# Splits of weights capped at two ahead of an operation, second feed-forward's first tiles interleaved, last mean first

## The chip, the core and the metric

The kernel runs on one NeuronCore of a Trainium2 chip. Its engines have an instruction queue each: PE multiplies matrices, ACT applies functions, DVE does elementwise arithmetic and reductions, POOL (GpSimd) a few helpers, SP issues most of the DMAs. Each works its own queue in order and waits for the others through semaphores. The metric is the device time of one execution in microseconds; lower is better.

## The reference

Two transformer blocks, one after the other, on 256 tokens of width 1024, in float32. Cut to what matters:

```python
mod = (silu(c) @ w_ada + b_ada).reshape(b, 3, 3, D)              # first block: shift, scale, gate per sub-layer
x = x + 0.5 * mod[0, 2] * swiglu(modulate(x, ...), w13[0], w2[0])  # first feed-forward, width 2816
x = x + mod[1, 2] * hybrid_mixer(modulate(x, ...))                 # latent attention, a convolution, gates, w_out
x = x + 0.5 * mod[2, 2] * swiglu(modulate(x, ...), w13[1], w2[1])  # second feed-forward
# second block
z = rmsnorm(x, g) @ w_in                                          # qa, ka, va, qb, kb, vb, two gates
x = x + (gate_a * (mixer_a(...) @ w_out_a) + gate_b * (mixer_b(...) @ w_out_b)) @ w_out
x = x + square(relu(rmsnorm(x, g) @ w_ff1)) @ w_ff2               # third feed-forward, width 4096
x = x + sigmoid(rmsnorm(x, g) @ w_ple_gate) * (p @ w_ple)
return rmsnorm(x, final_norm_g)
```

In the mixer `c_q`, `c_kv` and `k_rope` are columns of one product; queries and keys are made from their norms by `w_uq` and `w_ukv`, and are normed again by head before they are rotated.

## The kernel before

**Products in pieces.** PE multiplies in a rounded format (fp32r). To keep float32's precision, every weight is split into a rounded part (`whi`) and the rest (`wlo`), and so is every activation (`hh` and `hl`, or two halves of `SR`); a product is three matmuls (`mm3`, L462). The weights, some 200 MB, come as 331 pieces of at most 128x1024 elements, in the order in which PE takes them (class `Plan`). SP's queue loads two pieces with one DMA into one of four slots of `raw`. ACT then makes `whi` (`hi_to`, L1280 to L1287), DVE subtracts it from `raw` for `wlo` (`lo_to`, L1747 to L1755), and PE waits for that in `take` (L470). Both halves stand in a ring of `NP` = 6 pieces: ACT may write piece n only when PE is done with piece n - 6, and SP may load a slot again only when DVE has read it. A piece of 8 times 128 columns is 24 matmuls on PE.

**What sets the order.** Nothing schedules the splits at run time. `pe_program` is first run without emitting (its `count`, L477); at each signal that PE gives, it writes down in `split_at[key]` how many pieces may be split before and after the operation that waits for that key, from the pieces that PE has freed by then plus 6. `act_program` calls `hi_before(key)` ahead of an operation that waits for PE, `hi_after(key)` behind some. `dve_program` calls `lo_for(key)` likewise, and `after_act(key)`, which splits as many pieces as ACT had split by the time that it gave the key (`hi_at`), and then waits for ACT. All of these have a `most` with the default 99: they split to the ring's full. `lo_to(n)` in turn waits for ACT's `hi_done` of each piece.

**Stages around the change.** The first block's mixer runs from about 235 us: projections (`gate` tiles, then `c0`, `c1`), six more `gate` pieces (78 to 83), `uq` (84, 85), `ukv` (86), `cv` (87 to 98, convolution inputs, `back1` 3 to 8), and `gate` again (99 on). Between pieces 91 and 92 PE transposes the first 128 tokens' queries and keys, between 92 and 93 those of the other 128 (key `qkT`, with t, operand, half); DVE and ACT scale them out of PSUM by halves. DVE's loop over t norms and rotates queries and keys of one half of the tokens (`normed`).

The second feed-forward has 22 rows (`NT`). Tile r has a gate product and an up product; DVE scales both by the row `RB` (`g_in`, `u_in`), ACT applies silu (`sg`), DVE multiplies (`av`), ACT rounds that (`ah`), and DVE makes the rest (`a`); PE then multiplies them by a row piece of `w2`. PE does the gate and up products of tiles 0 to 3 before row 0. The buffers `W1`, `W2` hold three tiles.

At the end, after the third feed-forward, PE multiplies `ple` (pieces 321, 322; key ("ple", t, half)), sums the squares (`sums` 4), transposes `xT` back (two times eight), and takes the gate's pieces 323 to 330 in pairs. `token_rstd` (L1809) makes a mean and an inverse square root out of `sums` on DVE: one operation of 128x2 with the key `mean`, one of int32, seven small ones and a scaling.

Only the order of ACT's and DVE's instructions is changed; the orders of PE, SP and POOL are the same in both kernels.

## Time and profile before

| | |
|---|---|
| median of 3 runs | 1071.82 us (1071.53 to 1072.54) |
| profiled execution | 1072.67 us |
| its span | 1070.6 us |
| granted PE clock, mean | 0.985 |
| PE busy | 1029.1 us (96%) |
| DVE busy | 704.7 us (66%) |
| ACT busy | 538.2 us (50%) |

The profile is of one execution. The median stands 0.85 us under it. A clock of 1.00 is 2.4 GHz; the other level is 1.2 GHz. The page cuts the span into 40 slices, and in nearly all of them PE is at nine tenths or more; the stretches of interest are the few in which PE waits, and the splits on DVE there. Rows of a timeline that begin with the same operation are folded: "x6" is six instructions, and the time ahead of it is theirs together. The time in brackets is how long the engine stood idle before the row, and which instruction released it.

### The profile page before, as it was taken

To read this page: it belongs to the slowest core of one execution; us is meant where nothing else is said; L and a number is where in the kernel's file an instruction comes from. 1 tells how busy PE (TensorE), PEld (TensorE's weight loads), DVE (VectorE), ACT (ScalarE), POOL (GpSimd) and SP (SyncE) were. 2 spreads that over 40 slices of the span, in tenths; PEclk is the share of its full clock that TensorE was granted. 3 is DMA by queue.
4 is the path that set the end of the run, shared out by engine and by line. 5 is a ranking of instruction groups with operands and counts; after the bars stand their busy time and mean duration, and the time that the engine had idled before them with its cause. 6 is when DMAs were issued, how large, how long until landed. Compare 5 with 4: busy or idle time off the path is not lost.

```text
span 1070.6 us, 19826 instructions
## 1 busy us (share of the span) xinstructions
PE 1029.1 (96%) x8502; PEld 997.5 (93%) x8502; DVE 704.7 (66%) x1213; ACT 538.2 (50%) x903; POOL 39.0 (4%) x75
## 2 busy tenths in 40 slices
PE   5999999999989999799999999999999999999985
PEld 3899999988989999799999999999999999999975
DVE  3478886567686577677666778655467775555475
ACT  4453443445645555444444577554355564454543
POOL 5000000010000000000000000003000000000000
PEclk8999999999999999899999999999999999999988
DMA  9979889787553363567555456346157475555411
GB/s 305 379 261 331 293 317 333 266 276 239 165 159 118 122 200 102 202 243 275 183 191 188 128 187 209 117 137 159 60 168 231 163 236 197 186 169 197 159 40 40
DMA packets 144463, 212.27 MB, mean 198 GB/s; under 512 B 4259, under 2 KB 121239, under 8 KB 144376
## 3 DMA queue, kind: packets, MB, share of 16 engines
q1 hardware_dynamic: 138928, 194.40, 54.5%
q0 software_dynamic: 5184, 16.30, 4.8%
q8 instruction: 67, 1.10, 0.4%
q10 hardware_dynamic: 264, 0.31, 0.1%
q14 instruction: 20, 0.16, 0.0%
HBM read 209.88 MB, written 1.11 MB: 197 GB/s over the span
## 4 chain that ended last, share of the span: by engine, by line
PE 66%; issue 22%; DVE 5%; DMA 3%; ACT 2%; SPq 0%; POOL 0%; POOLq 0%; DVEq 0%; ACTq 0%
PE PS L460 65%; DMA SC<-in_w_ada_dram 3%; DVE wlo L1754 3%; PE PS L468 2%; ACT whi L1286 1%; DVE SC L1712 0%; DVE W L1712 0%; DVE xT L1721 0%; DVE st L1724 0%; ACT W L1273 0%; DVE hl L1721 0%; DVE SS L1712 0%; DVE st L1721 0%; DVE SC L1718 0%; ACT L1273 0%
## 5 line engine op out<-in xcount | busy, mean ns | idle before, releaser
L1754 DVE TENSOR_TENSOR wlo<-raw,whi 128x1024 fp32r<-128x1024 f32 (+2 forms) x331 | 385.4, 1187 | 218.7 <-ACT whi L1286 218.2
L1286 ACT ACTIVATE whi<-raw 128x1024 fp32r<-128x1024 f32 (+2 forms) x331 | 330.1, 1022 | 162.0 <-PE PS L460 125.4
L460 PE MATMUL PS<-hh,whi 128*128 128x256 f32 (+1 forms) x1376 | 394.2, 287 | 4.8 <-DVE wlo L1754 3.3
L460 PE MATMUL PS<-hh,wlo 128*128 128x256 f32 (+1 forms) x1376 | 389.2, 283 | 0.0
L460 PE MATMUL PS<-hl,whi 128*128 128x256 f32 (+1 forms) x1376 | 388.3, 282 | 0.0
L460 PE MATMUL PS<-SR,whi 128*128 128x256 f32 (+1 forms) x1824 | 330.9, 284 | 8.0 <-DVE W L1712 5.8
L460 PEld LDWEIGHTS PS<-SR,whi 128*128 128x128 f32 x1824 | 281.5, 189 | 12.5 <-DVE W L1712 6.0
L460 PEld LDWEIGHTS PS<-hh,whi 128*128 128x128 f32 x1376 | 260.6, 189 | 9.8 <-DVE wlo L1754 4.3
L460 PEld LDWEIGHTS PS<-hl,whi 128*128 128x128 f32 x1376 | 261.3, 190 | 0.4
L460 PEld LDWEIGHTS PS<-hh,wlo 128*128 128x128 f32 x1376 | 261.0, 190 | 0.0
L460 PE MATMUL PS<-SR,wlo 128*128 128x256 f32 (+1 forms) x912 | 257.8, 283 | 0.0
L460 PEld LDWEIGHTS PS<-SR,wlo 128*128 128x128 f32 x912 | 172.8, 190 | 0.0
L1278 ACT ACTIVATE SR<-W 128x256 fp32r<-128x256 f32 (+1 forms) x76 | 35.0, 461 | 93.6 <-DVE W L1721 51.9
L460 PE MATMUL PS<-whi,hh 128*128 128x256 f32 x240 | 69.4, 289 | 0.0
L460 PE MATMUL PS<-wlo,hh 128*128 128x256 f32 x240 | 68.1, 284 | 0.0
L460 PE MATMUL PS<-whi,hl 128*128 128x256 f32 x240 | 68.0, 283 | 0.0
L1712 DVE TENSOR_TENSOR SR<-W,SR 128x256 fp32r<-128x256 f32 (+1 forms) x76 | 36.5, 480 | 42.6 <-ACT SR L1278 42.6
L1273 ACT ACTIVATE W<-W 128x256 f32<-128x256 f32 (+1 forms) x38 | 21.3, 561 | 78.3 <-DVE W L1712 40.4
L460 PE MATMUL PS<-SC 128*64 128x128 f32 (+5 forms) x246 | 47.6, 336 | 0.0
L460 PEld LDWEIGHTS PS<-whi,hh 128*128 128x128 f32 x240 | 46.4, 193 | 0.6 <-DVE wlo L1754 0.4
L460 PEld LDWEIGHTS PS<-wlo,hh 128*128 128x128 f32 x240 | 46.4, 193 | 0.1
L460 PEld LDWEIGHTS PS<-whi,hl 128*128 128x128 f32 x240 | 46.3, 193 | 0.0
(183 smaller groups left out, 717.7 us busy)
## 6 DMA issues: line engine op xcount, KB each, us to landing
raw<-in_ffn_w_dram SPq DMA_DIRECT2D x60, 1024.0 KB, 5.5
raw<-in_w_in_dram SPq DMA_DIRECT2D x38, 1024.0 KB, 5.4
raw<-in_w_ff_dram SPq DMA_DIRECT2D x32, 1024.0 KB, 5.3
raw<-in_w_ada_dram SPq DMA_DIRECT2D x16, 1024.0 KB, 6.6
SC<-in_w_ada_dram POOLq DMA_DIRECT2D x12, 1024.0 KB, 5.8
SC<-in_w_ada_dram SPq DMA_DIRECT2D x8, 1024.0 KB, 12.0
raw<-in_w_out_dram SPq DMA_DIRECT2D x8, 1024.0 KB, 4.8
raw<-in_ffn_w_dram SPq DMA_DIRECT2D x8, 768.0 KB, 12.9
```

Source lines behind the costliest of these rows:

```text
L460: return e.matmul(o, l, r, start=start, stop=stop, skip_group_check=True)
L468: return e.transpose(o, i, ident[0:p, 0:p])
L1273: e.activation(o, i, f, bias=bias, scale=scale, accum_out=acc).then_inc(*act_done.up(*keys))
L1278: e.activation(o, i, ACT.Copy, scale=scale).then_inc(*act_done.up(*keys))
L1286: e.activation(hi_part(p), raw_part(p), ACT.Copy).then_inc(*hi_done.up(p.i))
L1712: e.tensor_tensor(o, x, y, op).then_inc(*dve_done.up(*keys))
L1754: e.tensor_tensor(lo_part(p), raw_part(p), hi32(hi_part(p)), ALU.subtract).then_inc(*lo_done.up(p.i))
```

## The change

- `split_at[key]` has a third number: how many pieces PE has already taken at that signal, which have to be split by then. `hi_before` and `lo_for` split these, and beyond them at most `most` pieces, now 2 by default, never past the ring's full. `lo_for` goes only as far as ACT had gone at its own `hi_before` of the same key (`high_by`); where ACT has none for the key, only the pieces already taken are left. `after_act` splits at most `most` (2) for all its keys together. Some calls have a `most` of 0 or 1.
- In the mixer the run of splits after each half's scaling (`lo_to(hi_at["qkT", 1, t])`) goes, and calls for ("ukv", t) and ("back1", 3 + t) come in.
- In the second feed-forward the steps of tiles 0, 1 and 2 are interleaved on ACT and DVE, and the up product is scaled right behind the gate product in all tiles.
- In the third feed-forward ACT may split behind the square.
- The last mean and root (`token_rstd(4, 3)`) stand ahead of the copies of `ple`, and a split between these.

```diff
--- before.py
+++ after.py
@@ -325,7 +325,7 @@
         every_signal = [mm_done, hi_done, lo_done, act_done, dve_done, pool_done, *raw_in, *row_in, *pair_in, c_in, *x_in, sv_in,
                         rel_in, hot_in, pos_in, sw_in, inv_in, cs_in, gb_in, rel_out, pin_in, gfin_in, out_done,
                         *out_lo, *bias_in]
-        split_at, hi_at = {}, {}
+        split_at, hi_at, high_by = {}, {}, {}
 
         def hi32(v):
             return v.bitcast(F32)
@@ -480,7 +480,7 @@
                 while used["free"] in used["done"]:
                     used["free"] += 1
                 for k in keys:
-                    split_at[k] = before, used["free"] + NP
+                    split_at[k] = used["n"], before, used["free"] + NP
                 return mm_done.up(*keys)
 
             def halves(p, k):
@@ -1286,11 +1286,12 @@
                     e.activation(hi_part(p), raw_part(p), ACT.Copy).then_inc(*hi_done.up(p.i))
                     high["n"] += 1
 
-            def hi_before(key, most=99):
-                hi_to(min(split_at[key][0], high["n"] + most))
-
-            def hi_after(key, most=99):
-                hi_to(min(split_at[key][1], high["n"] + most))
+            def hi_before(key, most=2):
+                hi_to(max(split_at[key][0], min(split_at[key][1], high["n"] + most)))
+                high_by[key] = high["n"]
+
+            def hi_after(key, most=2):
+                hi_to(min(split_at[key][2], high["n"] + most))
 
             def modulated(s, ks, free=None, ahead=(), piece_key=None):
                 for k in ks:
@@ -1531,16 +1532,29 @@
             hi_before(("g", 1, 0))
             on.wait_ge(mm_done, ("rstd_row", 2))
             copy(RB[:, 0:S], PS[:, 1, 0:S], ("RB", 2))
-            for r in range(NT):
+            def gate_on(r):
                 hi_before(("g", 1, r))
                 on.wait_ge(dve_done, ("g_in", 1, r))
                 sg = W1[:, r % 3, :]
                 func(sg[:, 0:S], sg[:, 0:S], ACT.Silu, ("sg", 1, r), bias=sg[:, S:S + 1])
                 hi_before(("u", 1, r))
+
+            def high_activated(r):
                 on.wait_ge(dve_done, ("av", 1, r))
                 if r >= 6:
                     on.wait_ge(mm_done, ("row", 1, r - 6))
                 copy(aring[r % 6][0], W2[:, r % 3, 0:S], ("ah", 1, r))
+
+            gate_on(0)
+            gate_on(1)
+            hi_before(("u", 1, 2))
+            high_activated(0)
+            gate_on(2)
+            high_activated(1)
+            high_activated(2)
+            for r in range(3, NT):
+                gate_on(r)
+                high_activated(r)
             ada_rows_out(8, 6, 0, ("ada_sum", 8))
             hi_before(("row", 1, NT - 4))
             for n in range(8):
@@ -1667,6 +1681,7 @@
                 hi_before(("f", j, 1))
                 on.wait_ge(dve_done, ("f_in", j))
                 func(W2[:, j % 3, :], W1[:, j % 3, :], ACT.Square, ("f_sq", j))
+                hi_after(("f", j, 1))
                 if j >= 4:
                     on.wait_ge(mm_done, ("row", 3, 2 * j - 7))
                 on.wait_ge(act_done, ("f_sq", j))
@@ -1754,12 +1769,11 @@
                     e.tensor_tensor(lo_part(p), raw_part(p), hi32(hi_part(p)), ALU.subtract).then_inc(*lo_done.up(p.i))
                     low["n"] += 1
 
-            def lo_for(key, most=99):
-                lo_to(min(split_at[key][0], low["n"] + most))
-
-            def after_act(*keys):
-                for k in keys:
-                    lo_to(hi_at[k])
+            def lo_for(key, most=2):
+                lo_to(max(split_at[key][0], min(high_by.get(key, 0), low["n"] + most)))
+
+            def after_act(*keys, most=2):
+                lo_to(min(max(hi_at[k] for k in keys), low["n"] + most))
                 on.wait_ge(act_done, *keys)
 
 
@@ -2140,22 +2154,24 @@
                 vcopy(k_sb[:, t, :, 64:96], kr.to_broadcast([128, HEADS, 32]), ("kr", t))
             lo_to(hi_at["back1", 2])
             for t in range(2):
-                after_act(("k_raw", t))
+                lo_for(("ukv", t), 1)
+                after_act(("k_raw", t), most=1)
                 src = PS[:, 4 + 2 * t:6 + 2 * t, :].rearrange("p g (h c) -> p g h c", h=4)
                 vcopy(v_sb[:, t, :].rearrange("p (g h c) -> p g h c", g=2, h=4), src[:, :, :, 64:128], ("k_in", t))
             for t in range(2):
-                after_act(("q_sq", t))
+                after_act(("q_sq", t), most=0)
                 qs = W1f[:, 768 * t:768 * t + 768].rearrange("p (h c) -> p h c", c=QKD)
                 reduce(ssq[:, 0, t, :], qs[:, :, 0:64], ALU.add)
                 reduce(ssq[:, 2, t, :], qs[:, :, 64:96], ALU.add)
             for t in range(2):
-                after_act(("k_sq", t))
+                after_act(("k_sq", t), most=0)
                 reduce(ssq[:, 1, t, :], W2f[:, 512 * t:512 * t + 512].rearrange("p (h c) -> p h c", c=64), ALU.add)
             last_one()
             ts(st[:, 88:120], st[:, 40:72], 1.0 / 64, EPS, ALU.mult, ALU.add)
             ts(st[:, 120:136], st[:, 72:88], 1.0 / 32, EPS, ALU.mult, ALU.add)
             rsqrt(st[:, 88:136], st[:, 136:184], st[:, 184:232], st[:, 40:88])
             for t in range(2):
+                lo_for(("back1", 3 + t), 1)
                 def of_head(a_, n):
                     return rs1[:, a_, t, :].unsqueeze(2).to_broadcast([128, HEADS, n])
 
@@ -2167,11 +2183,10 @@
                 tt(k_sb[:, t, :, 0:64], k_sb[:, t, :, 0:64], of_head(1, 64), ALU.mult, ("normed", 1, t))
             for t in range(2):
                 for i, (dst, g) in enumerate(((qT, gq96), (kT, gk96))):
-                    lo_for(("qkT", t, i, 0))
+                    lo_for(("qkT", t, i, 0), 1)
                     on.wait_ge(mm_done, ("qkT", t, i, 0))
                     ts1(dst[:, 0:4, 128 * t:128 * t + 128], PS[0:96, 4 + 2 * i, :].rearrange("p (h c) -> p h c", h=4), g, ALU.mult,
                         ("qkT", i, t))
-                lo_to(hi_at["qkT", 1, t])
                 if t:
                     read_back1([3, 4])
 
@@ -2231,25 +2246,44 @@
             lo_for(("sums", 1))
             token_rstd(1, 0)
             spread_rstd(1, ("rstd_row", 1))
-            for r in range(NT):
+            def gate_and_up(r):
                 sg, av = W1[:, r % 3, :], W2[:, r % 3, :]
                 g, u = ((4, 5), (6, 7), (2, 3))[r] if r < 3 else (4, 5) if r % 2 else (6, 7)
                 lo_for(("g", 1, r))
                 if r == 0:
-                    after_act(("RB", 2))
+                    after_act(("RB", 2), most=0)
                     on.wait_ge(pool_done, "one")
                 on.wait_ge(mm_done, ("g", 1, r))
                 if r >= 3:
                     on.wait_ge(dve_done, ("a", 1, r - 3))
                 tt(sg[:, 0:S + 1], PS[:, g, 0:S + 1], RB[:, :], ALU.mult, ("g_in", 1, r))
-                lo_for(("u", 1, r))
+                lo_for(("u", 1, r), 0)
                 on.wait_ge(mm_done, ("u", 1, r))
                 tt(av[:, 0:S + 1], PS[:, u, 0:S + 1], RB[:, :], ALU.mult, ("u_in", 1, r))
+
+            def activated(r):
+                sg, av = W1[:, r % 3, :], W2[:, r % 3, :]
                 after_act(("sg", 1, r))
-                last_one()
+                on.wait_ge(dve_done, ("u_in", 1, r))
                 stt(av[:, 0:S], av[:, 0:S], av[:, S:S + 1], sg[:, 0:S], ALU.add, ALU.mult, ("av", 1, r))
+
+            def low_activated(r):
                 after_act(("ah", 1, r))
-                tt(aring[r % 6][1], av[:, 0:S], hi32(aring[r % 6][0]), ALU.subtract, ("a", 1, r))
+                tt(aring[r % 6][1], W2[:, r % 3, 0:S], hi32(aring[r % 6][0]), ALU.subtract, ("a", 1, r))
+
+            gate_and_up(0)
+            gate_and_up(1)
+            activated(0)
+            gate_and_up(2)
+            activated(1)
+            low_activated(0)
+            activated(2)
+            low_activated(1)
+            low_activated(2)
+            for r in range(3, NT):
+                gate_and_up(r)
+                activated(r)
+                low_activated(r)
             after_act(("ada_rows", 8))
             lo_for(("ada_col", 8))
             mod_half(8, 6, 0)
@@ -2402,11 +2436,12 @@
 
 
 
-            lo_for(("ple", 1, 1))
-            for t in range(2):
+            lo_for(("ple", 1, 1), 0)
+            token_rstd(4, 3)
+            for t in range(2):
+                lo_for(("ple", t, 1), 1)
                 on.wait_ge(mm_done, ("ple", t, 0))
                 vcopy(ple[:, t, 0:512], PS[:, 4 + 2 * t, :], ("ple", t))
-            token_rstd(4, 3)
             on.wait_ge(gfin_in, "gfin")
             for u in range(4):
                 for t in range(2):
```

The rows below are DVE's instructions in the order of its queue. `wlo<-raw,whi` is the low half of a piece; "x2" is two instructions alike. The first place is the mixer's loop over the two halves of the tokens, where products with `st` are norms and those with `rtab` rotations, and 96x4x128 is the scaling of transposed queries and keys. Before:

```order
L1712 TENSOR_TENSOR SC<-SC,rtab 128x8x32
L1712 TENSOR_TENSOR SC<-SC,W2 128x8x32
L1712 TENSOR_TENSOR SC<-SC,st 128x8x64
L1712 TENSOR_TENSOR SC<-SC,st 128x8x32
L1712 TENSOR_TENSOR SC<-SC,st 128x8x64
L1712 TENSOR_TENSOR W2<-SC,rtab 128x8x16 x2
L1712 TENSOR_TENSOR SC<-SC,rtab 128x8x32
L1712 TENSOR_TENSOR SC<-SC,W2 128x8x32
L1712 TENSOR_TENSOR SC<-SC,st 128x8x64
L1754 TENSOR_TENSOR wlo<-raw,whi 128x1024 x6
L1718 TENSOR_SCALAR SC<-PS,svt 96x4x128 x2
L1754 TENSOR_TENSOR wlo<-raw,whi 128x1024
```

After:

```order
L1727 TENSOR_TENSOR SC<-SC,rtab 128x8x32
L1727 TENSOR_TENSOR SC<-SC,W2 128x8x32
L1727 TENSOR_TENSOR SC<-SC,st 128x8x64
L1769 TENSOR_TENSOR wlo<-raw,whi 128x1024 x2
L1727 TENSOR_TENSOR SC<-SC,st 128x8x32
L1727 TENSOR_TENSOR SC<-SC,st 128x8x64
L1727 TENSOR_TENSOR W2<-SC,rtab 128x8x16 x2
L1727 TENSOR_TENSOR SC<-SC,rtab 128x8x32
L1727 TENSOR_TENSOR SC<-SC,W2 128x8x32
L1727 TENSOR_TENSOR SC<-SC,st 128x8x64
L1769 TENSOR_TENSOR wlo<-raw,whi 128x1024
L1733 TENSOR_SCALAR SC<-PS,svt 96x4x128 x2
```

The six low halves ahead of the scalings (pieces 92 to 97) are gone; two (89 and 90) stand behind the first half's norm, one (91) ahead of the scalings. Before, 89 to 91 stood ahead of this stretch, together with 88.

The second place is the start of the second feed-forward, from the spread of the root (`sm<-ones,sm`). `W1<-PS,RB` and `W2<-PS,RB` are the gate's and the up product's scaling, `W2<-W2,W1` their product, `SR<-W2,SR` its low half. Before:

```order
L1715 TENSOR_SCALAR sm<-ones,sm 128x128 x2
L1712 TENSOR_TENSOR W1<-PS,RB 128x257
L1754 TENSOR_TENSOR wlo<-raw,whi 128x1024
L1712 TENSOR_TENSOR W2<-PS,RB 128x257
L1721 SCALAR_TENSOR_TENSOR W2<-W2,W1 128x256
L1712 TENSOR_TENSOR SR<-W2,SR 128x256
L1754 TENSOR_TENSOR wlo<-raw,whi 128x1024
L1712 TENSOR_TENSOR W1<-PS,RB 128x257
L1754 TENSOR_TENSOR wlo<-raw,whi 128x1024
L1712 TENSOR_TENSOR W2<-PS,RB 128x257
L1721 SCALAR_TENSOR_TENSOR W2<-W2,W1 128x256
L1712 TENSOR_TENSOR SR<-W2,SR 128x256
```

After:

```order
L1730 TENSOR_SCALAR sm<-ones,sm 128x128 x2
L1769 TENSOR_TENSOR wlo<-raw,whi 128x1024 x2
L1727 TENSOR_TENSOR W1<-PS,RB 128x257
L1727 TENSOR_TENSOR W2<-PS,RB 128x257
L1769 TENSOR_TENSOR wlo<-raw,whi 128x1024 x2
L1727 TENSOR_TENSOR W1<-PS,RB 128x257
L1727 TENSOR_TENSOR W2<-PS,RB 128x257
L1736 SCALAR_TENSOR_TENSOR W2<-W2,W1 128x256
L1769 TENSOR_TENSOR wlo<-raw,whi 128x1024 x2
L1727 TENSOR_TENSOR W1<-PS,RB 128x257
L1727 TENSOR_TENSOR W2<-PS,RB 128x257
L1736 SCALAR_TENSOR_TENSOR W2<-W2,W1 128x256
```

The scalings of three tiles now come before the third product, and the first low half of an activation stands behind the third tile's scalings.

The third place is the last mean, `sm<-PS`; `SC<-PS 128x512` is a copy of `ple`. Before:

```order
L1721 SCALAR_TENSOR_TENSOR hl<-xT,svt,hh 128x256
L1754 TENSOR_TENSOR wlo<-raw,whi 128x1024 x3
L1709 COPY SC<-PS 128x512 x2
L1715 TENSOR_SCALAR sm<-PS 128x2
L1715 TENSOR_SCALAR sm<-sm 128x2
L1721 SCALAR_TENSOR_TENSOR sm<-sm 128x1 x2
L1721 SCALAR_TENSOR_TENSOR sm<-sm 128x2
L1721 SCALAR_TENSOR_TENSOR sm<-sm 128x1 x2
L1721 SCALAR_TENSOR_TENSOR sm<-sm 128x2 x2
L1718 TENSOR_SCALAR sm<-sm 128x2
L1754 TENSOR_TENSOR wlo<-raw,whi 128x1024 x2
```

After:

```order
L1736 SCALAR_TENSOR_TENSOR hl<-xT,svt,hh 128x256
L1730 TENSOR_SCALAR sm<-PS 128x2
L1730 TENSOR_SCALAR sm<-sm 128x2
L1736 SCALAR_TENSOR_TENSOR sm<-sm 128x1 x2
L1736 SCALAR_TENSOR_TENSOR sm<-sm 128x2
L1736 SCALAR_TENSOR_TENSOR sm<-sm 128x1 x2
L1736 SCALAR_TENSOR_TENSOR sm<-sm 128x2 x2
L1733 TENSOR_SCALAR sm<-sm 128x2
L1724 COPY SC<-PS 128x512
L1769 TENSOR_TENSOR wlo<-raw,whi 128x1024
L1724 COPY SC<-PS 128x512
L1769 TENSOR_TENSOR wlo<-raw,whi 128x1024 x3
```

The mean and the root went ahead of all splits and copies; the piece that PE takes with the first pair (324) stands behind them and one copy.

## Rows read from the trace of the kernel before

**Rows 1.** The page: busy time and share, PE.

```profile
PE 1029.1 (96%) x8502; PEld 997.5 (93%) x8502; DVE 704.7 (66%) x1213; ACT 538.2 (50%) x903; POOL 39.0 (4%) x75
```


**Rows 2.** The page: the chain that ended last, by engine.

```profile
PE 66%; issue 22%; DVE 5%; DMA 3%; ACT 2%; SPq 0%; POOL 0%; POOLq 0%; DVEq 0%; ACTq 0%
```


**Rows 3.** The page: the splits' low halves, 331; busy and mean ns, idle before.

```profile
L1754 DVE TENSOR_TENSOR wlo<-raw,whi 128x1024 fp32r<-128x1024 f32 (+2 forms) x331 | 385.4, 1187 | 218.7 <-ACT whi L1286 218.2
```


**Rows 4.** Waits of PE from 60 us on: total, times, longest (us).

```profile
PE PS L460 <- DVE W L1712: 5.8, 1, 5.8
PE PS L468 <- DVE sm L1715: 5.2, 1, 5.2
...
PE PS L460 <- DVE wlo L1754: 0.4, 1, 0.4
```


**Rows 5.** Timeline of PE: start us, us, what, [idle before <- releaser].

```profile
266.24 0.39 PE L460 MATMUL PS<-hh,whi 128*128 128x256 f32 x1 [1.01 <-DVE SC L1718]
...
290.99 0.28 PE L460 MATMUL PS<-hh,wlo 128*128 128x256 f32 x1
...
299.67 1.91 PE L468 MATMUL PS<-ident,SC 128*96 128x128 f32 x16
...
308.39 3.33 PE L468 MATMUL PS<-ident,SC 128*96 128x128 f32 x16 [3.31 <-DVE SC L1718]
...
439.82 0.79 PE L460 MATMUL PS<-SR,whi 128*128 128x256 f32 x2 [5.83 <-DVE W L1712]
```


**Rows 6.** Windows: length, busy of PE, PEld, DVE, ACT, POOL, clock, DMA.

```profile
300.00:320.00 20.00, 16.30 (x124) 15.65 (x123) 16.79 (x25) 10.46 (x17) 0.00 (x0) 0.91 0.68 211
440.00:460.00 20.00, 20.00 (x151) 20.00 (x152) 14.54 (x20) 9.55 (x14) 0.00 (x0) 0.89 0.63 223
```


**Rows 7.** Timeline of DVE in the first block's mixer.

```profile
234.21 3.10 DVE L1754 TENSOR_TENSOR wlo<-raw,whi 128x1024 fp32r<-128x1024 f32 x3
238.68 0.16 DVE L1715 TENSOR_SCALAR sm<-PS 128x2 f32<-128x2 f32 x1 [1.37 <-PE PS L460]
...
240.64 0.48 DVE L1715 TENSOR_SCALAR sm<-ones,sm 128x128 f32<-128x128 f32 x2
...
284.61 3.50 DVE L1754 TENSOR_TENSOR wlo<-raw,whi 128x1024 fp32r<-128x1024 f32 x3 [5.51 <-ACT whi L1286]
...
296.98 1.75 DVE L1712 TENSOR_TENSOR SC<-SC,st 128x512 f32<-128x512 f32 x3
...
300.69 6.89 DVE L1754 TENSOR_TENSOR wlo<-raw,whi 128x1024 fp32r<-128x1024 f32 x6
307.50 1.40 DVE L1718 TENSOR_SCALAR SC<-PS,svt 96x512 f32<-96x512 f32 x2
...
316.13 1.22 DVE L1754 TENSOR_TENSOR wlo<-raw,whi 128x1024 fp32r<-128x1024 f32 x1
```


**Rows 8.** Timeline of DVE in the projections by token.

```profile
637.36 2.35 DVE L1754 TENSOR_TENSOR wlo<-raw,whi 128x1024 fp32r<-128x1024 f32 x2
```


**Rows 9.** Timeline of DVE at the second feed-forward's start.

```profile
422.89 0.43 DVE L1712 TENSOR_TENSOR W<-PS,RB 128x257 f32<-128x257 f32 x1 [1.22 <-ACT RB L1278]
...
436.27 0.42 DVE L1712 TENSOR_TENSOR W<-PS,RB 128x257 f32<-128x257 f32 x1
...
439.35 0.42 DVE L1712 TENSOR_TENSOR W<-PS,RB 128x257 f32<-128x257 f32 x1
```


**Rows 10.** Timeline of PE at the last mean.

```profile
1027.41 1.07 PE L468 MATMUL PS<-ident,xT 128*128 128x128 f32 x8
1033.63 1.97 PE L468 MATMUL PS<-ident,xT 128*128 128x128 f32 x8 [5.16 <-DVE sm L1715]
```


**Rows 11.** Timeline of DVE at the last mean.

```profile
1028.82 3.50 DVE L1754 TENSOR_TENSOR wlo<-raw,whi 128x1024 fp32r<-128x1024 f32 x3 [1.79 <-ACT whi L1286]
1032.23 1.28 DVE L1709 COPY SC<-PS 128x512 f32<-128x512 f32 x2
1033.43 0.15 DVE L1715 TENSOR_SCALAR sm<-PS 128x2 f32<-128x2 f32 x1
```


## The prediction

> **What bounds the kernel now.** I read the profile's page first. PE is busy 96% of the span [rows 1], and the chain that ended last is PE for 66% and issue for 22% [rows 2], so what counts is each microsecond in which PE stands still or runs at the lower clock. DVE and ACT have room on average: a piece of weights, once ACT has rounded it, takes DVE 1.19 us for what is left [rows 3], against 24 matmuls at 0.119 us, 2.85 us, on PE. So an edit of DVE's or ACT's order costs nothing unless PE arrives at a piece whose split is not there. Then the waits of PE behind the opening stage: 5.8 us once on the products of the second feed-forward, 5.2 us once on the last mean, 0.4 us once on a split [rows 4]; the others are in PE's timeline below: 3.3 us once on the scaled queries, and a few of 1 us or less. These are where a gain can lie.
>
> The windows and PE's timeline say what a stall costs beyond its length. After 1.01 us of idle at 266.24 the next matmuls keep their 0.12 us pace; after 3.31 us at 308.39 sixteen transposes take 3.33 us where sixteen took 1.91 at 299.67, so 1.4 us more; after 5.83 us at 439.82 the window 440:460 shows a granted clock of 0.89 with PE never idle: 11% of 20 us, 2.2 us [rows 5, 6]. There are two levels, 2.4 and 1.2 GHz, and half the time spent at the lower is lost. I price a stall of 1 us at its length, one of 5 to 6 us at its length plus 1.7 (between 1.4 and 2.2), and one of 2 us with 0 to 1.4 more, taking 0.6.
>
> **First block's mixer: the cap takes splits out of slack.** Before, DVE split to the end of the ring of six wherever it might. Now at most two come ahead of an operation, and for a key at which ACT never asked (("back1", 3), ("qkT", t, i, 0)) only the pieces that PE has already taken. Five places come out of it.
> - Piece 73: before, DVE split 73 to 75 in 234.21 to 237.31 and then had 1.37 us idle before the mean at 238.68; mean, root and spread end at 241.1 [rows 7]. Now the split stands behind them and ends at 241.1 + 1.2 = 242.3, where PE wants it at about 240.8: +1.5. In return the five splits that held the root of the latent's norm go behind it, and the stall of 1.01 [rows 5] goes: together +0.5.
> - Piece 85: it now stands behind the rotation of the keys (two rounds, about 2.0 us of small operations); PE wants it 1.4 us sooner: +1.4.
> - Piece 89, the largest: before, 89 to 91 were split at 284.61 to 288.11, in an idle of 5.51 us, ahead of the copies, squares' sums, root and first rotation that end with the 296.98 row's first operation (0.68 us: 297.66) [rows 7]. Now 89 and 90 stand behind that. ACT asks two pieces instead of three before its copies (-0.95) but starts 1.4 later, so the chain ends at 298.1 and the split at 299.3. PE finishes piece 88 at 291.27 [rows 5] + 1.9 from the two items above = 293.2: a stall of 6.1, and 1.7 of clock, +7.8.
> - Piece 92: behind the first two scalings (0.70 each, 1.40 for both at 307.50), [rows 7], the second of which waits for the third quarter of the transposes, a quarter of 1.91 us before PE wants the piece: 0.70 + 1.2 - 0.48 = 1.4.
> - Piece 93: before, split in the run of six at 300.69, now where piece 99 stood: behind both scalings, the sum with ACT's copy and four products, which ended so that its split ran at 316.13 for 1.22 us, to 317.35 [rows 7]. The second sixteen transposes ended at 308.39 + 3.33 = 311.72, after which PE wants the piece: 5.6, and 1.7 of clock, +7.3.
> - Gone: that run of six (6.89 us) ahead of the scalings, so the 3.31 stall, its 1.4 of clock, and the 0.4 at piece 92 [rows 4]: -5.1.
>
> Sum 0.5 + 1.4 + 7.8 + 1.4 + 7.3 - 5.1 = +13.3. Ends: +10 if the chain before 89 starts 2 us sooner and the clock falls once, +17 if the shorter stalls too cost clock.
>
> **Second block's projections by token.** The pairs of splits at 637.36 (2.35 us) and after are in the same place, but each now trails a rotation by one piece more [rows 8]. I get 0.5 at the keys, 1.6 at the queries and 0.2 to 0.5 at a turn, +2.3; from 0 (each has a row of DVE idle of 0.5 to 2.8 us within 10 us before it) to +4.
>
> **Start of the second feed-forward.** Before, each of the first tiles r goes DVE, ACT, DVE, ACT, DVE in turn; from tile 0's first scaling at 422.89 to tile 2's at 436.27 are two rounds, 6.69 us each, and PE waits until tile 2's second scaling at 439.35 is done [rows 9]. Now both scalings of tile 1 and then of tile 2 come between the steps of tile 0. In the durations of [rows 9]: spread, two splits (2.4), scalings of 0 (0.8), two splits, scalings of 1, a product, two splits, scalings of 2: 421.7 + 7.2 (six splits) + 2.5 + 0.5 = about 431.7, and the tile 0 product's low half near 433.5. PE is ready at 433.99 before, and 0.3 earlier as the spread moves ahead of a split. So the stall of 5.83 and its 2.2 of clock go [rows 5, 6]: -8.3, between -5 (2.8 us left, with clock) and -8.8. Later tiles have 14 us of room per piece: the cap costs nothing there.
>
> **The way into the third feed-forward** has a 0.94 stall of which half stays: -0.5.
>
> **The last mean.** Before, DVE ran three splits at 1028.82 and two copies at 1032.23 before the mean at 1033.43, and PE idled 5.16 us ahead of the second eight transposes [rows 10, 11]. Now the mean goes at once, 1027.6, and the transposes go on to 1029.3. Then PE wants piece 324, whose split is behind mean and root (1.83, the rows' 1033.43 to 1035.26) and one copy (0.6): 1027.6 + 1.83 + 0.6 + 1.2 = 1031.3. So a stall of 2.0 takes the place of 5.16: the gate's matmuls start at 1031.3 instead of 1035.26, -3.95, and at 0.119 instead of 0.213 us until 1038.4, up to 1.4 more. I take -4.6; the tail of 11 us after the last piece keeps its length.
>
> A rule bears on that 1.4. Before, eight transposes on the way took 1.97 us after the stall against 1.07 before it [rows 10]. The Trainium skill, "TensorE: Matmul & The Clock Gate", Part 4 (PE-mode transpose), says that a transpose does not count as busy for the clock gate. By that rule the transposes and the 2.0 us behind them are one quiet stretch, the gate's matmuls start slow as before, and this part gives -4.0 rather than -5.4. No row here shows transposes followed by a stall of this length.
>
> **Sum.** 13.3 + 2.3 - 8.3 - 0.5 - 4.6 = +2.2 us. The profiled execution took 1072.67, so 1074.9 in its terms; it stood 0.85 above the median of 1071.82, so I predict 1074.0 in the terms of the median. By the ends: 1071.82 + 10 + 0 - 8.8 - 0.5 - 5.4 = 1067.1, and 1071.82 + 17 + 4 - 5 - 4 = 1083.8.
>
> **Rivals.**
> 1. Faster: the front gives less. The by-token pairs fall into their idle (-2.3), piece 85 is hidden behind the longer run of PE (-1.4), and the clock does not fall a second time at piece 93 (-1.7): 1068.6. For it: DVE is busy for 66% only, and 16.79 of 20 us in the window 300:320 held 8 splits that now leave it. Against: 89 and 93 stand behind long serial chains whatever the load.
> 2. Slower: each new stall of 1.4 to 2 us lowers the clock as well. Four places at 1.1 each: 1078.4. For it: 3.31 us did. Against: 1.01 us did not. It decides from where between the two the clock falls.
> 3. Slower: the interleaving leaves half of the 5.8 us, since tile 0's last product waits behind six splits and tile 2 behind ACT's; 3 us stay, with the 2.2 of clock: 1079.2. Against: each of the splits was there before too, in the idle time of the DVE.
> 4. The change does nothing for the mixer, because a piece that PE has taken and one that it is about to take differ by one position only: then +2.2 - 13.3, 1060.7. Against: the order of DVE's instructions has piece 89 behind the whole norm.
>
> **Chances.** Forecast (1071 to 1077) 0.42; rival 1 0.25; rival 2 0.17; rival 3 0.10; rival 4 and the rest 0.06. A measurement can tell about 0.2% from no change, so faster means below 1069.7 and slower above 1074.0. Faster: three quarters of rival 1, and rival 4: 0.22. Same: the rest of rival 1 and half of the forecast: 0.27. Slower: the rest, 0.51. The range leaves out rival 4 and the far part of rival 3: 1067.5 to 1079.5; the forecast's own is 1071 to 1077.
>
> **What would show it.** PE waits of 5 to 6.5 us on a split twice between 290 and 325, with clocks under 1 in two windows there; waits of 1 to 2 us at the two short places before and at 640; no wait over 1 us at the start of the second feed-forward and window 440:460 at 1.00; at the end one wait of 2 us on a split. The prediction is wrong if the wait at piece 89 is under 4 us or if a stall over 2 us remains at 434.

## The result, and the profile after

| | before | changed |
|---|---|---|
| median | 1072.18 us (1071.53 to 1073.11, 4 runs) | 1083.24 us (1082.89 to 1085.34, 4 runs) |
| ratio | | 1.0107, 95% interval [1.0089, 1.0124] |
| profiled execution, its span | 1072.67, 1070.6 | 1083.11, 1081.1 |
| granted PE clock, mean | 0.985 | 0.981 |

The change makes the kernel 11 us slower. The forecast was 2 us slower, with a range up to 1079.5, so the time lies outside. The page of the changed kernel shows PE busy for the same share of the span and DVE for a little less (64% for 66%); as before [rows 1, 3], averages say nothing here:

```profile
PE 1033.6 (96%) x8502; PEld 999.4 (92%) x8502; DVE 696.9 (64%) x1213; ACT 531.7 (49%) x903; POOL 39.1 (4%) x75
```

The view of PE's waits from 60 us on answers to [rows 4]. Total, times and longest are in us:

```profile
PE PS L460 <- DVE wlo L1769: 24.0, 12, 5.9
```

The three long waits of before (5.8, 5.2, 3.3 us, each on another result) are gone. In their place stand twelve on one thing, the low half of a piece. PE's timeline of the changed kernel has them one by one, and answers to [rows 5, 10]:

```profile
91.62 0.58 PE L460 MATMUL PS<-hh,whi 128*128 128x256 f32 x1 [2.68 <-DVE wlo L1769]
...
99.61 0.39 PE L460 MATMUL PS<-hh,whi 128*128 128x256 f32 x1 [0.62 <-DVE wlo L1769]
...
103.23 0.39 PE L460 MATMUL PS<-hh,whi 128*128 128x256 f32 x1 [0.52 <-DVE wlo L1769]
...
248.34 0.50 PE L460 MATMUL PS<-SR,whi 128*128 128x258 f32 x2 [1.41 <-DVE wlo L1769]
...
286.58 0.42 PE L460 MATMUL PS<-whi,SR 128*128 128x384 f32 x1 [1.61 <-DVE wlo L1769]
...
294.16 0.39 PE L460 MATMUL PS<-hh,whi 128*128 128x256 f32 x1 [0.31 <-DVE wlo L1769]
...
305.97 0.58 PE L460 MATMUL PS<-hh,whi 128*128 128x256 f32 x1 [5.86 <-DVE wlo L1769]
...
319.74 0.39 PE L460 MATMUL PS<-hh,whi 128*128 128x256 f32 x1 [1.54 <-DVE wlo L1769]
...
330.29 0.58 PE L460 MATMUL PS<-hh,whi 128*128 128x256 f32 x1 [5.69 <-DVE wlo L1769]
...
649.70 0.39 PE L460 MATMUL PS<-whi,hh 128*128 128x256 f32 x1 [0.44 <-DVE wlo L1769]
...
656.99 0.39 PE L460 MATMUL PS<-whi,hh 128*128 128x256 f32 x1 [1.38 <-DVE wlo L1769]
...
1045.57 0.36 PE L460 MATMUL PS<-whi,hh 128*128 128x256 f32 x1 [1.98 <-DVE wlo L1769]
```

The rows from 248 on are pieces 73, 85, 87, 89, 92 and 93, two of the projections by token, and 324, all places that the prediction names except 87. The first three, in the first feed-forward, are in no term of it. The windows tell where the clock was low, as in [rows 6]; 440:460, which stood at 0.89 before, is at 1.00:

```profile
80.00:100.00 20.00, 16.70 (x127) 16.30 (x126) 9.93 (x13) 3.64 (x5) 0.00 (x0) 0.91 0.45 153
300.00:320.00 20.00, 12.61 (x92) 12.24 (x91) 13.34 (x27) 3.64 (x6) 0.00 (x0) 0.83 0.18 54
320.00:340.00 20.00, 14.31 (x106) 13.96 (x106) 10.70 (x18) 10.47 (x17) 0.00 (x0) 0.83 0.35 105
440.00:460.00 20.00, 19.88 (x167) 19.70 (x166) 15.29 (x25) 11.61 (x18) 0.00 (x0) 1.00 0.43 158
1040.00:1060.00 20.00, 18.02 (x136) 17.54 (x135) 13.63 (x28) 9.47 (x17) 0.00 (x0) 0.91 0.00 1
```

I then took the same operations of PE in both traces, since PE's order is the same, and noted by how much the changed kernel is later at each (the up product of the first feed-forward's tile 8 ends at 106.35, before at 100.35: 6.0). The lateness grows and shrinks in steps. The second feed-forward is counted from the spread of its root on, as in the prediction:

| place | lateness at its end, us | step | forecast |
|---|---|---|---|
| first feed-forward, tiles 7 and 8 | 6.0 | +6.0 | none |
| first block's mixer | 20.4 | +14.3 | +13.3 |
| start of the second feed-forward, with its spread | 12.0 | -8.4 | -8.3 |
| projections by token | 14.9 | +2.9 | +2.3 |
| into the third feed-forward | 14.2 | -0.7 | -0.5 |
| last mean | 10.4 | -3.8 | -4.6 |

Before rounding the steps add up to 10.4; the spans differ by 10.5.

A stall makes PE later by about 0.25 us more than its idle time, also where the clock does not fall: the wait of 1.41 us is a step of 1.66, that of 1.38 a step of 1.64. The rows show why. At full pace a matmul lasts 0.28 us and the next one starts 0.12 us after it, so the idle time is counted from an end that lies 0.16 us behind the next start, and the first matmul behind a stall lasts up to 0.39 us and not 0.28.

**What happened in the first feed-forward.** ACT's timeline of the kernel before, from 73 to 92 us: it rounds four pieces in a row (22 to 25) and then waits 7.2 us for a load. The two loads that bring pieces 26 to 29 are issued from 81.73 on, when DVE has made the low halves of 24 and 25 (the first line, from SP's timeline).

```profile
81.73 1.50 SPq L1198 DMA_DIRECT2D raw<-in_ffn_w_dram  x2
...
75.88 3.90 ACT L1286 ACTIVATE whi<-raw 128x1024 fp32r<-128x1024 f32 x4
86.97 1.06 ACT L1286 ACTIVATE whi<-raw 128x1024 fp32r<-128x1024 f32 x1 [7.20 <-DMA raw<-in_ffn_w_dram]
90.49 2.01 ACT L1286 ACTIVATE whi<-raw 128x1024 fp32r<-128x1024 f32 x2 [2.45 <-DMA raw<-in_ffn_w_dram]
```

ACT's timeline of the changed kernel, the same stretch: two pieces (22, 23), then it stands idle for 11.1 us in front of the silu of tile 6, which waits for PE's product out of piece 23. Only then are 24 and 25 rounded, when PE already wants 24.

```profile
75.89 2.00 ACT L1286 ACTIVATE whi<-raw 128x1024 fp32r<-128x1024 f32 x2
88.98 0.38 ACT L1273 ACTIVATE W<-PS 128x256 f32<-128x256 f32 x1 [11.10 <-PE PS L460]
89.26 1.99 ACT L1286 ACTIVATE whi<-raw 128x1024 fp32r<-128x1024 f32 x2
...
96.72 1.06 ACT L1286 ACTIVATE whi<-raw 128x1024 fp32r<-128x1024 f32 x1 [5.17 <-DMA raw<-in_ffn_w_dram]
100.86 1.06 ACT L1286 ACTIVATE whi<-raw 128x1024 fp32r<-128x1024 f32 x1 [3.07 <-DMA raw<-in_ffn_w_dram]
```

The rest follows down the line. DVE, which waits for ACT's half, makes the low halves of 24 and 25 late; with each of them a slot of `raw` comes free, so SP issues the next two loads from 91.60 on and not from 81.73:

```profile
90.34 2.36 DVE L1769 TENSOR_TENSOR wlo<-raw,whi 128x1024 fp32r<-128x1024 f32 x2 [0.52 <-ACT whi L1286]
...
91.60 1.50 SPq L1198 DMA_DIRECT2D raw<-in_ffn_w_dram  x2
```

So ACT rounds piece 26 at 96.72 (before: 86.97) and 27 at 100.86 (before: 90.49). PE pays 2.68 us, 1.7 us of lower clock and of restart, then 0.62 and 0.52, and 0.5 for these two restarts: 6.0. Tile 6 is the first whose gate and up products come from the stream of pieces; those of tiles 0 to 5 come from the opening pieces 0 to 15, long done when ACT asks. Why the cap costs nothing more in the tiles behind 8 stays open.

### The profile page after: what moved, and what is told of

Same layout as the page of the kernel before. It is cut to its first block, busy times and chain, and to the rows that moved or that the text cites. A ratio compares the mean times of both kernels' runs of the same rounds, so it can differ in the third digit from the quotient of the medians.

```text
span 1081.1 us, 19808 instructions
## 1 busy us (share of the span) xinstructions
PE 1033.6 (96%) x8502; PEld 999.4 (92%) x8502; DVE 696.9 (64%) x1213; ACT 531.7 (49%) x903; POOL 39.1 (4%) x75
## 4 chain that ended last, share of the span: by engine, by line
PE 68%; issue 22%; DVE 6%; DMA 2%; ACT 2%; SPq 0%; POOL 0%; POOLq 0%; DVEq 0%
PE PS L460 66%; DVE wlo L1769 2%; PE PS L468 2%; DMA SC<-in_w_ada_dram 1%; DMA raw<-in_ffn_w_dram 1%; DVE SC L1727 1%; ACT SC L1278 1%; ACT whi L1286 1%; DVE xT L1736 0%; DVE W L1727 0%; DVE hl L1736 0%; DVE st L1739 0%; ACT W L1273 0%; DVE SS L1727 0%; DVE SC L1724 0%
## 5 line engine op out<-in xcount | busy, mean ns | idle before, releaser
L1727 DVE TENSOR_TENSOR W<-PS,RB 128x257 f32<-128x257 f32 x44 | 18.0, 423 | 46.7 <-PE PS L460 45.4
```

What stands on the lines that cost most here:

```text
L1727: e.tensor_tensor(o, x, y, op).then_inc(*dve_done.up(*keys))
```

## The experiments

Each ran beside the kernel before, so a ratio stands beside every time. The time of the kernel before differed between the occasions: its median was 1072.2 us beside the changed kernel, 1073.2 beside e1 to e4, 1073.6 beside e5 to e8 and 1073.7 beside e9 and e10. The expectations were written in plain times, so these are compared first; where it matters, the difference by the ratios stands beside them, in us of 1072.2. Base is either the changed kernel or the kernel before. The diffs show the lines that matter, with dots for the others. Theory A throughout: the places don't influence each other, and each costs what its stall and its clock cost.

**e1: the first feed-forward's splits uncapped.** The changed kernel with a switch; where it is on, `hi_before`, `hi_after`, `lo_for` and `after_act` take the limits of before. It is on around ACT's loop, shown here, and around DVE's.

```diff
+            full["on"] = True
             for r in range(NT):
                 swiglu0(r)
...
+            full["on"] = False
             on.wait_ge(dve_done, (("h", 0), 7))
```

> The changed kernel, but with the splits of the first feed-forward (ACT and DVE) to the ring's full, as before the change. Theory A (the costs of the places are independent and add up): the stalls of 2.68, 0.62 and 0.52 us that the changed kernel shows between 91 and 104 us, and the 1.7 us at the lower clock behind the first, go, and nothing takes their place: about 1083.2 - 6.0 = 1077.2 us, with all the later stalls unchanged. Rival B (the cap's lateness is passed on: a stall that goes at one place comes back at the next one, since DVE and ACT are as late as before): less than half of it comes back, 1080.5 or more.

Measured: 1077.01 us (1075.56 to 1078.66, 8 runs), ratio to before 1.0037 [1.0025, 1.0049]. That is 6.2 us less than the changed kernel (7.5 by the ratios, 1.0107 and 1.0037, with an interval of 5.2 to 9.8, which holds the 6.0). In its profile nothing is waited for between 60 and 240 us, and the other waits on pieces are as they were (PE, all from 60 us on: nine instead of twelve):

```profile
PE PS L461 <- DVE wlo L1776: 20.2, 9, 5.9
```

The same operations of PE are 6.0 us earlier than in the changed kernel behind this place. Farther on the two profiles differ by their clock alone, with the same waits: 1.0 us more is lost to it in the mixer and 1.5 us less at the last mean. So the missing term is this one, and rival B falls: nothing is passed on.

**e2: the mixer's splits as before.** The same switch around the mixer, on ACT too; there the run behind the scalings comes back, and the new calls for ("ukv", t) and ("back1", 3 + t) drop out.

```diff
+            full["on"] = True
             lo_for(("sums", 0))
             token_rstd(0, 0)
...
+                lo_to(hi_at["qkT", 1, t])
                 if t:
                     read_back1([3, 4])
+            full["on"] = False
```

> The changed kernel, but with the splits of the first block's mixer, from its first mean to the second half's scalings, in the order of before the change. Theory A: stalls of 1.41, 1.61, 0.31, 5.86, 1.54 and 5.69 us go and the ones of before (1.01, 0.38, 3.31) return with their clock: 13.8 us less, 1083.2 - 13.8 = 1069.4 us, so faster than the kernel before. Rival B: half of it or less, 1076 or more.

Measured: 1070.25 us (1066.93 to 1073.46, 10 runs), ratio 0.9972 [0.9959, 0.9985]: 13.0 us less than the changed kernel, 14.5 by the ratios. The forecast was 13.8 less, so A holds and B falls. The stalls of before came back (1.01, 0.38, 3.31), with one new wait of 0.43 us at 254.18. The profiled execution is the fastest of the ten, and odd in its clock, told of at the end.

**e3: the interleaving alone**, on the kernel before. ACT's and DVE's loops over the first three tiles are those of the changed kernel, the splits go to the ring's full; only the call between the gate's and the up product's scaling is left out (the changed kernel has it with a `most` of 0).

```diff
-            for r in range(NT):
...
+            gate_and_up(0)
+            gate_and_up(1)
+            activated(0)
+            gate_and_up(2)
+            activated(1)
+            low_activated(0)
...
```

> The kernel before with one part of the change alone: the first three tiles of the second feed-forward interleaved on ACT and DVE, every split to the ring's full as before. Theory A: the 5.8 us wait and its 2.2 us at the lower clock go, 1072.2 - 7.8 = 1064.4 us (between 1063.8 and 1065). Rival C (the interleaving pays only since the cap keeps the splits out of these steps): the third tile's scaling is still late behind the splits to the ring's full, 2 to 3 us of the wait stay, with the lower clock: 1067 to 1069.

Measured: 1063.86 us (1062.62 to 1064.59, 4 runs), ratio 0.9911 [0.9894, 0.9927]. The 5.8 us wait is gone from its list of waits, of which the first four are:

```profile
PE PS L468 <- DVE sm L1728: 5.2, 1, 5.2
PE PS L468 <- DVE SC L1731: 3.3, 1, 3.3
PE PS L460 <- DVE SC L1731: 1.0, 1, 1.0
PE PS L460 <- DVE xT L1725: 0.9, 1, 0.9
```

Rival C falls: the interleaving doesn't need the cap of two. DVE's timeline of e3 shows two splits between the tiles, as in the changed kernel, although `most` is unlimited: DVE waits for ACT's half at each pair (1.19 and 0.80 us), so ACT has no more pieces to give there.

```profile
423.21 0.76 DVE L1725 TENSOR_TENSOR W<-PS,RB 128x257 f32<-128x257 f32 x2 [1.22 <-ACT RB L1278]
425.16 2.36 DVE L1767 TENSOR_TENSOR wlo<-raw,whi 128x1024 fp32r<-128x1024 f32 x2 [1.19 <-ACT whi L1286]
427.44 0.75 DVE L1725 TENSOR_TENSOR W<-PS,RB 128x257 f32<-128x257 f32 x2
428.11 0.48 DVE L1734 SCALAR_TENSOR_TENSOR W<-W 128x256 f32<-128x256 f32 x1
429.38 2.36 DVE L1767 TENSOR_TENSOR wlo<-raw,whi 128x1024 fp32r<-128x1024 f32 x2 [0.80 <-ACT whi L1286]
431.66 0.75 DVE L1725 TENSOR_TENSOR W<-PS,RB 128x257 f32<-128x257 f32 x2
```

The third tile's scalings end at 432.4, where they ended at 439.8 before [rows 9]; the prediction had 431.7.

**e4: the last mean alone**, on the kernel before.

```diff
-            lo_for(("ple", 1, 1))
+            token_rstd(4, 3)
             for t in range(2):
                 on.wait_ge(mm_done, ("ple", t, 0))
                 vcopy(ple[:, t, 0:512], PS[:, 4 + 2 * t, :], ("ple", t))
-            token_rstd(4, 3)
+                if not t:
+                    lo_for(("ple", 1, 1), 1)
+            lo_for(("ple", 1, 1))
```

> The kernel before with another part of the change alone: the last mean and root ahead of the copies and splits. Theory A: the 5.2 us wait becomes one of 2.0 us on piece 324, and the clock falls all the same: 1072.2 - 3.9 = 1068.3 us. Rival D (the clock falls because of the length of the gap alone, and 2.0 us are not enough): no matmul at the lower pace behind it, 1.5 us more: 1066.8.

Measured: 1068.44 us (1067.28 to 1070.67, 5 runs), ratio 0.9961 [0.9945, 0.9977]. The wait of 5.16 became one of 1.98 us, and the lower pace is there (PE's timeline; from 1031.09 on each matmul lasts 0.41 us and not 0.28, and the next one starts 0.21 us later and not 0.12):

```profile
1026.61 1.94 PE L468 MATMUL PS<-ident,xT 128*128 128x128 f32 x16
1030.53 0.35 PE L460 MATMUL PS<-whi,hh 128*128 128x256 f32 x1 [1.98 <-DVE wlo L1754]
1030.73 0.28 PE L460 MATMUL PS<-wlo,hh 128*128 128x256 f32 x1
...
1030.96 0.33 PE L460 MATMUL PS<-whi,hh 128*128 128x256 f32 x1
1031.09 0.41 PE L460 MATMUL PS<-wlo,hh 128*128 128x256 f32 x1
```

So A holds here, in time (1068.3) and in the clock. Rival D's price, no fall of the clock behind the same gap, is seen in the profiles of e1 and e2; the last section has both.

**e5 and e10: both gains on the kernel before**, with the mean's operation alone first and the root behind the copies.

```diff
...
+            ts(sm[:, 272:272 + n], PS[:, 3, 0:n], 1.0 / D, EPS, ALU.mult, ALU.add, ("mean", 4))
             for t in range(2):
                 on.wait_ge(mm_done, ("ple", t, 0))
                 vcopy(ple[:, t, 0:512], PS[:, 4 + 2 * t, :], ("ple", t))
+                if not t:
+                    lo_for(("ple", 1, 1), 1)
+            last_one()
+            rsqrt_columns(sm[:, 272:272 + n], rsy[:, 0:n], sm[:, 276:276 + n], n)
...
```

> The kernel before with the two paying parts: the tiles of the second feed-forward interleaved, and at the end the mean alone first (one operation), then a copy, the split of piece 324, the other copy, and only then the root. Theory A (the stalls add up, and at the end PE waits for piece 324 and not for the root): the wait ahead of the gate's matmuls is 0.7 us instead of 2.0, so 1063.9 (interleaving alone) - 4.7 (last mean alone) - 1.3 = 1057.9 us, and 1056.4 if the clock no longer falls. Rival: the root is needed there after all, or the piece's high half is late; then the wait stays near 2 us: 1059.2.

> The kernel of e5_both_gains once more, unchanged, on the chip of the run beside it, for comparison: 1057.6 us.

Measured: 1057.58 us (1056.79 to 1058.98, 4 runs), ratio 0.9850 [0.9835, 0.9866]; again, on another occasion, 1058.88 us, ratio 0.9866 [0.9843, 0.9888]. PE's wait ahead of the gate's matmuls is 0.80 us (forecast 0.7):

```profile
1022.86 0.36 PE L460 MATMUL PS<-whi,hh 128*128 128x256 f32 x1 [0.80 <-DVE wlo L1767]
```

PE needs the mean only since it has to be read before the second eight transposes overwrite it. The root is needed by ACT, which first reads it 5.7 us after the mean (1025.98 for 1020.29) and waits there for PE, not for DVE. The changed kernel put the whole chain ahead. In both profiles the matmuls behind the 0.80 us keep the full pace, and for that case A had 1056.4; in plain times the two runs stand 1.2 and 2.5 us above it, by the ratios (1056.1 and 1057.8) at it and 1.4 above. This rest is unexplained.

**e6: the keys that ACT doesn't have.** The changed kernel, the cap as it is; for the keys ("back1", 3) and ("qkT", ...) the limit is the ring's, not 0.

```diff
-                lo_to(max(split_at[key][0], min(high_by.get(key, 0), low["n"] + most)))
+                lo_to(max(split_at[key][0], min(high_by.get(key, split_at[key][1] if key[0] == "qkT" or key == ("back1", 3) else 0), low["n"] + most)))
```

> The changed kernel, where lo_for has for the keys (back1, 3) and (qkT, t, i, 0), at which ACT never asked, the old limit instead of 0; the cap stays at two or one pieces. It puts piece 89 ahead of the first half's norm instead of behind it, and pieces 93 and 94 between the second half's scalings. Theory A (the two long stalls of the mixer come from the keys that ACT doesn't have, not from the size of the cap): piece 89's wait 5.86 - 3.1 (norm and rotation of a half) = 2.8, piece 92's 0.8, piece 93's gone with its 1.7 us of clock: 11.2 to 12.9 us less, 1070.3 to 1072.0. Rival E (the cap of two itself is what delays them): the waits move to the pieces behind, less than 5 us gained, 1078 or more.

Measured: 1073.76 us (1072.06 to 1074.84, 10 runs), ratio 0.9999 [0.9990, 1.0008]. In plain times that is 9.5 us less than the changed kernel and 1.8 us above the upper end of A; by the ratios it is 11.6 us less, which is inside A (11.2 to 12.9). Rival E falls either way. PE's timeline has the waits for pieces 89, 91 and 92:

```profile
302.60 0.39 PE L460 MATMUL PS<-hh,whi 128*128 128x256 f32 x1 [2.76 <-DVE wlo L1769]
...
310.85 0.39 PE L460 MATMUL PS<-hh,whi 128*128 128x256 f32 x1 [0.78 <-DVE wlo L1769]
...
316.37 0.38 PE L460 MATMUL PS<-hh,whi 128*128 128x256 f32 x1 [0.66 <-DVE wlo L1769]
```

Piece 89 is as A has it (2.76 for 2.8), and so is 92 (0.66 for 0.8, behind the first transposes at 313.79). Piece 93's wait is gone. A had not counted piece 91, which now waits 0.78 us, nor two waits of 0.3 us on ACT in the attention. Set side by side, PE's operations in the two profiles give 11.6 us for pieces 89, 92 and 93, less 1.0 for piece 91 and 1.3 for the attention: 9.3 of the mixer's 14.3. The larger part of the mixer's loss, then, is not the number two: it is that a key unknown to ACT gives DVE nothing beyond what PE has taken already.

**e7: a filler.** e4, and 16 matmuls whose result is overwritten, between the two sets of transposes.

```diff
                 if t:
+                    for k in range(KD):
+                        on.wait_ge(dve_done, (("xs1", 4), k))
+                        for i in range(2):
+                            mm(PS[:, 2, 0:256], hh[:, k, 0:128], hh[:, k, 0:256], True, True)
                     on.wait_ge(dve_done, ("mean", 4))
```

> The kernel with the last mean alone moved (e4_last_mean_only) and 16 matmuls of 128x256 with no use between the two sets of eight transposes; their result is overwritten. They fill the 1.98 us in which PE waited for piece 324 (16 x 0.119 = 1.9). Theory F (transposes and the gap together lower the clock): the gate's matmuls stay at 0.119 us, and 1068.4 - 1.5 = 1066.9 us. Rival G (the fall has another cause than idle time and transposes): 1068.4, with the lower pace still there. If they delay the transposes more than they fill: 1069 or more.

Measured: 1067.63 us (1066.50 to 1069.72, 6 runs), ratio 0.9946 [0.9931, 0.9961] against e4's 0.9961 [0.9945, 0.9977]. The intervals overlap, so the time decides nothing. In its profile no wait is left there and the gate's matmuls go at 0.12 us from the start; but see the last section for why one profile doesn't decide it.

**e8 and e9: a cap only where a run stands ahead of what PE waits for.** e5, with

```diff
-            lo_for(("ada_col", 6))
+            lo_for(("ada_col", 6), 4)
...
-            after_act("c_sq")
+            on.wait_ge(act_done, "c_sq")
...
-                    lo_for(("qkT", t, i, 0))
+                    lo_for(("qkT", t, i, 0), 2 if (t, i) == (0, 0) else 0)
...
-                lo_to(hi_at["qkT", 1, t])
+                lo_to(min(hi_at["qkT", 1, t], low["n"] + 3))
```

(this is e9; e8 has no 4 in the first call, so that piece 83 is still split ahead of the root and the 1.01 us wait stays, and a 2 instead of the 3).

> The kernel of e5_both_gains, and in the mixer a cap only where a run of splits stands ahead of what PE waits for: two splits instead of six ahead of the first half's scalings, two behind each half's, and the sum of squares' root not behind piece 83. Theory A: the waits of 1.0 and 3.3 us go and at most 0.5 us comes instead; 4.3 us less than e5, and 1.4 more where the clock fell: 1052.2 to 1053.6 us. Rival B: the pieces held back are late themselves (94 to 98), as those of the changed kernel were, and half or more comes back: 1055.5 or more.

> The kernel of e8_mixer_trimmed with two corrections: piece 83 is now split behind the root of the latent's norm (in e8 another call still split it ahead, and the 1.01 us wait stayed), and three pieces instead of two are split behind each half's scalings, so that one less stands ahead of the first scores, where e8 showed new waits of 1.06 and 1.03 us. Theory A: the wait at 266 goes (-1.0) and of the 2.4 us of new waits at least 1 goes: 1056.3 - 2.0 = 1054.3 us. Rival B (what is taken from one queue place is late at the next): the sum of the waits between 260 and 335 us stays near 3.8 us, 1056.3.

Measured: e8 1056.32 us (1055.86 to 1057.12, 4 runs), ratio 0.9838 [0.9824, 0.9852]. e9 1055.91 us (1055.47 to 1056.35, 4 runs), ratio 0.9835 [0.9818, 0.9853], the fastest of all, 3.0 us under e10 beside it. The intervals of these two ratios touch, but the times themselves, four of each, do not: 1055.47 to 1056.35 against 1058.00 to 1060.07. Those of e8 and e5, again beside each other, do (1055.86 to 1057.12, 1056.79 to 1058.98), so e8's gain is not clear of noise. For e8 the time is rival B's (1055.5 or more), but not its cause: in the mixer PE waits for one low half, 0.39 us, as it did before, and for none of the pieces that are held back. E9 lies nearer B's 1056.3 than A's 1054.3; of A's two steps the first came (the wait at 266 is gone) and the second did not. PE's timeline of e9 in the mixer's attention:

```profile
320.55 0.55 PE L468 MATMUL PS<-ident,SC 128*128 128x128 f32 x3 [1.05 <-DVE SC L1731]
...
325.64 0.52 PE L468 MATMUL PS<-ident,SC 128*128 128x128 f32 x3 [1.03 <-ACT SC L1278]
...
330.97 0.52 PE L468 MATMUL PS<-ident,SC 128*128 128x128 f32 x3 [0.33 <-ACT SC L1278]
```

The waits of 1.0 and 3.3 us are gone, and 2.4 us of new ones stand in the attention, on results of DVE and ACT, which PE now reaches sooner. The third split behind the scalings changed none of them (1.06, 1.03, 0.32 in e8). Their cause stays open, and so does whether a split's place could shorten them.

## Why the prediction was wrong, step by step

- **The missing step: the first feed-forward.** The prediction has no term for it; it costs the cap in "later tiles" of the second one at nothing, by their 14 us of room, and says of the first nothing at all. It cost +6.0, and e1, which undoes that place alone, gives 6.2 back. The room was there in the first one as well, for DVE and ACT as a sum; what was not counted is that an in-order engine that waits for PE can't use it. The silu stands in front of the splits, and it waits for the product out of the last piece that had been split. With this term the forecast is 1074.0 + 6.0 = 1080.0, 3.2 us under the measured 1083.2. The other steps together were 2.2 off (the table, before rounding: 1.0 - 0.1 + 0.6 - 0.1 + 0.8), the median of before went from 1071.8 to 1072.2, and the medians differ by 11.1 where the spans differ by 10.5.
- **The mixer** was right in mechanism and nearly in size: 14.3 against 13.3. Piece 73: 1.41 (1.5). 85: 1.61 (1.4). 89: 5.86 (6.1). 92: 1.54 (1.4). 93: 5.69 (5.6). Piece 87's 0.31 was overlooked, and so was the 0.25 us that a stall costs beyond its length: three more stalls than before make 0.75. Undone alone (e2), it gives 13.0 in plain times, 14.5 by the ratios.
- **The second feed-forward's start:** -8.4 against -8.3. Of it 7.8 are the stall with its clock (forecast 8.0) and 0.6 the spread (0.3). Alone, it gives 9.5 us by e3's ratio, whose interval reaches from 7.8 to 11.4.
- **By token:** +2.9 against +2.3; the waits are 0.44 and 1.38 (0.5 and 1.6), each with 0.25 for the restart.
- **The last mean:** -3.8 against -4.6. The wait was 1.98 (2.0). The term that was off is the clock: I took 0.6 us of the 1.4 as won, and in that profile nothing of it was.
- **Rivals.** Rival 1 (less in the front) and 3 (half of the 5.8 stays) are refuted by the waits, rival 4 by pieces 89 and 93. Rival 2 is on the side where the time went, for another reason: the waits of 1.4 to 1.6 us lowered no clock (the granted clock behind each stays at 1.00, and the steps are about 0.25 us over the waits), the one of 2.68 did.
- **The range** did not hold the time, though the ends of the terms, 1067.1 to 1083.8, do. The upper end needed every part at its worst: 17 in the mixer, 4 by token, 3.3 us of the second feed-forward's gain lost. Each of these stayed short of it, and the 6.0 us that stood in no term made up for them, so it is chance that 1083.2 lies under 1083.8. The range itself was narrower, to 1079.5, since it left out rival 4 and the far part of rival 3. Neither the ends nor the rivals had a term for the first feed-forward.
- **The signs** named in advance came: the two long waits (the second at 330 and not by 325, with the 6 us ahead of it), the short ones, the window at 1.00 and the wait of 2 us. They tested the terms of the sum and could not show one that was missing.

## What to carry to other kernels

When a limit is put on work done ahead, walk the whole program for it, stage by stage, and ask at each operation that waits for the bottleneck engine: are the inputs of that engine's next two steps already made by what stands in front? Free time on the limited engine is no cover if it lies behind that wait. Where two engines prepare the same work by keys, check that every key one of them uses exists for the other; here a silent default of 0 cost 9.3 us by e6's profile, more than the 6.0 of the first feed-forward. And move ahead only the one operation that is waited for: the mean without its root was worth 1.2 us of stall more than the mean with it.

## What the runs showed of the hardware

Whether a gap lowers PE's clock is not the same in each execution of the same code. A gap of 3.31 to 3.33 us ahead of sixteen transposes is in seven profiles. In six of them the transposes take 3.33 (before), 2.80 (e3), 3.22 (e4), 3.46 (e5), 3.44 (e7) and 3.42 us (e10), and in one (e2) 1.92, the full pace:

```profile
315.13 1.92 PE L469 MATMUL PS<-ident,SC 128*96 128x128 f32 x16 [3.31 <-DVE SC L1740]
```

Likewise the gap of 1.98 us behind sixteen transposes: the lower level (1.2 GHz) follows in the changed kernel, in e4 and in e6, but not in e1 and e2, whose windows there stand at 1.00. In the changed kernel it follows 1.5 us after PE is back at work, not at once (in e6 1.5 us too, in e4 0.6 us):

```profile
1046.82 0.28 PE L460 MATMUL PS<-wlo,hh 128*128 128x256 f32 x1
1046.94 0.31 PE L460 MATMUL PS<-whi,hl 128*128 128x256 f32 x1
1047.06 0.41 PE L460 MATMUL PS<-whi,hh 128*128 128x256 f32 x1
```

The rule weighed in the prediction is that transposes don't count as busy for the clock gate (the Trainium skill, "TensorE: Matmul & The Clock Gate", Part 4, PE-mode transpose). The lower level comes in three profiles and not in two, with the same operations and the same gap. So the rule stays open; its price for the last mean, -4.0 us, was nearer to the measured -3.8 than the -4.6 taken. What the profiles show is that 2.0 us of gap with 1.9 us of transposes ahead are enough at times, that 2.68 us (changed kernel, e2, e6) and 2.76 us (e6) between matmuls alone were enough in all four cases, and that gaps of 1.35 to 1.62 us between matmuls never were, in any of these profiles. With e7's filler the pace stayed full in one profile, but so it did without it in e1 and e2. It also means that a single profile prices a gap of 2 to 3.3 us with an error of about 1.5 us (1.92 against 3.46 us for sixteen transposes; 1.5 us between e1 and the changed kernel at the last mean). The ten runs of e2 lie between 1066.9 and 1073.5 us; how much of that is the clock, no run shows.
